# Attention scores of both heads issued together, one head in each half of TensorE's rows

## The reference

```
# stick-breaking, per head and block of 128 queries
z = q @ k.T * scale;  mask = key_pos < q_pos
log_beta = log_sigmoid(z);  log_1m = where(mask, log_sigmoid(-z), 0)
suffix = cumsum(log_1m, reverse=True) - log_1m
out = where(mask, exp(log_beta + suffix), 0) @ v
# global
out = softmax(q @ k.T * scale) @ v
# window: 128 keys to either side, bias by distance, one sink logit a head
s = q @ k.T * scale + bias;  m = max(max(s), sink);  p = exp(s - m)
out = (p / (sum(p) + exp(sink - m))) @ v
# neighbourhood: per grid row of 64 tokens, all 8 rows' keys in 16 columns
out = softmax(q @ k.T * scale + rpb[...]) @ v
```

## Time and profile before

| | us |
|---|---|
| median of 3 runs | 2117.64 (2117.27 to 2120.7) |
| profiled execution | 2116.69 |
| its span, first to last instruction | 2114.8 |
| PE busy | 2027.3 (96%), 8940 matmuls |
| VectorE busy | 1150.7 (54%) |
| ScalarE busy | 804.2 (38%) |
| GpSimd busy | 131.6 (6%) |
| mean granted TensorE clock | 0.980 |

### The profile page before, as it was taken

How to read it: one execution, slowest core, us unless ns; L and a number is a source line. 1 busy time by engine, 2 the same in 40 slices (tenths; PEclk the granted TensorE clock), 3 DMA queues, 4 the chain that set the end, 5 groups by cost and what they waited for, 6 DMA issues and landing times.

```text
span 2114.8 us, 26021 instructions
## 1 busy us (share of the span) xinstructions
PE 2027.3 (96%) x8940; PEld 1529.5 (72%) x8940; DVE 1150.7 (54%) x1991; ACT 804.2 (38%) x1402; POOL 131.6 (6%) x223
## 2 busy tenths in 40 slices
PE   6998999999999999999999997999898999999987
PEld 6875888888886665788888885565576866675766
DVE  6576534334456667444434465667754457677543
ACT  5456422222334445332212342544533333344331
POOL 1100000000000000000000000000003024342000
PEclk9998999999999999999999998999999999999998
DMA  6422232323321111223322320111222223222221
GB/s 215 148 80 70 90 100 92 117 80 98 100 87 54 58 52 50 82 90 99 109 81 98 102 88 31 40 55 50 65 68 84 79 68 79 69 75 65 79 73 69
DMA packets 48346, 173.78 MB, mean 82 GB/s; under 512 B 7344, under 2 KB 9408, under 8 KB 48016
## 3 DMA queue, kind: packets, MB, share of 16 engines
q1 hardware_dynamic: 41184, 160.45, 23.1%
q0 software_dynamic: 7088, 12.37, 2.4%
HBM read 168.58 MB, written 4.21 MB: 82 GB/s over the span
## 4 chain that ended last, share of the span: by engine, by line
PE 88%; DVE 7%; ACT 3%; issue 2%; DMA 1%; POOL 0%; DVEq 0%; ACTq 0%; SPq 0%; POOLq 0%
PE ps L366 25%; PE ps L368 23%; PE ps L367 23%; PE ps L458 7%; PE ps L488 3%; PE ps L466 3%; PE ps L549 1%; DVE Wl L1055 1%; PE ps L475 1%; ACT Wh L719 1%; DVE stat L1184 1%; DVE scr L1181 1%; DMA nmask<-in_nmask 1%; PE ps L435 0%; PE ps L401 0%
## 5 line engine op out<-in xcount | busy, mean ns | idle before, releaser
L366 PE MATMUL ps<-Hh,Wh 128*128 128x512 f32 x1568 | 641.4, 409 | 0.0
L368 PE MATMUL ps<-Hh,Wl 128*128 128x512 f32 x1568 | 613.3, 391 | 0.0
L367 PE MATMUL ps<-Hl,Wh 128*128 128x512 f32 x1568 | 612.9, 391 | 0.0
L719 ACT ACTIVATE Wh<-Wr 128x1024 fp32r<-128x1024 f32 (+2 forms) x276 | 308.9, 1119 | 709.1 <-PE ps L368 696.6
L1055 DVE TENSOR_TENSOR Wl<-Wr,Wh 128x1024 fp32r<-128x1024 f32 (+2 forms) x276 | 359.5, 1302 | 254.5 <-ACT Wh L719 254.4
L366 PEld LDWEIGHTS ps<-Hh,Wh 128*128 128x128 f32 x1568 | 294.7, 188 | 140.9 <-issue 84.2
L368 PEld LDWEIGHTS ps<-Hh,Wl 128*128 128x128 f32 x1568 | 294.8, 188 | 64.6
L367 PEld LDWEIGHTS ps<-Hl,Wh 128*128 128x128 f32 x1568 | 295.4, 188 | 55.4 <-issue 0.7
L366 PE MATMUL ps<-Yh,Wh 128*128 128x512 f32 (+1 forms) x800 | 305.0, 381 | 30.5 <-DVE Yl L1085 16.6
L367 PE MATMUL ps<-Yl,Wh 128*128 128x512 f32 (+1 forms) x800 | 301.0, 376 | 0.0
L368 PE MATMUL ps<-Yh,Wl 128*128 128x512 f32 (+1 forms) x800 | 300.5, 376 | 0.0
(11 more groups left out here) (175 smaller groups left out, 1596.2 us busy)
## 6 DMA issues: line engine op xcount, KB each, us to landing
Wr<-in_w SPq DMA_DIRECT2D x228, 512.0 KB, 3.4
Wr<-in_w SPq DMA_DIRECT2D x32, 768.0 KB, 4.2
Wr<-in_w SPq DMA_DIRECT2D x16, 640.0 KB, 3.9
scr<-in_rpb POOLq DMA_DIRECT2D x128, 24.0 KB, 2.0
X<-in_x SPq DMA_DIRECT2D x1, 2048.0 KB, 13.8
scr<-in_wri POOLq DMA_DIRECT2D x4, 512.0 KB, 3.8
out_t<-X SPq DMA_DIRECT2D x8, 256.0 KB, 2.1
scr<-d_rel POOLq DMA_DIRECT2D x8, 192.0 KB, 3.4
```

Source lines behind the costliest of these rows:

```text
L366: pe.matmul(bank[:, 0:n], hi, rh[:, k, :], start=(k == 0), stop=False)
L367: pe.matmul(bank[:, 0:n], hi, rl[:, k, :], start=False, stop=False)
L368: return pe.matmul(bank[:, 0:n], lo, rh[:, k, :], start=False, stop=(k == kc - 1))
L719: act.activation(Wh[:, slot, 0:kc * P], Wr[:, slot, 0:kc * P], ACT.Copy).then_inc(w_hi, 1)
```

## The change

Steps are reordered: `head_block` makes step `j` head `j % 2` and block `j // 2` (the memory attention keeps its order and gets a function of its own, `mem_scores`, with the wait of before). `scores` does nothing in an odd step; in an even one it issues the scores of both heads, head 0 in the array's rows 0 to 63 into `ps[2]`, head 1 in rows 64 to 127 into `ps[3]`, 512 keys as two cuts of 256. It waits for the exp of step g-1 (`t_e` at g), in the window stage for the bias add of step g-1. `Em` gets a second buffer by the parity of the pair, laid into `sq` and `ht`, so that GpSimd may write a pair's masks when the pair two before is done.

```
+def head_block(kind, j):
+    return (j // 4, j % 4) if kind == MEMA else (j % 2, j // 2)
...
-        Em = part(10240 + 2 * BW, 2, 8 * 112)
+        Em0 = part(10240 + 2 * BW, 2, 8 * 112)
+        Em = [[Em0[:, 0, :], Em0[:, 1, :]], [sq.rearrange("p a b -> p (a b)")[:, 0:8 * 112],
+                                             ht.rearrange("p a b -> p (a b)")[:, 0:8 * 112]]]
...
-            def mask_bias(i, hp):
+            def mask_bias(i, hp, par):
                 pool.wait_ge(en_in[hp], 128 * i + 128)
-                pool.wait_ge(sb_ok, 8 * i + (28 + 4 * hp))
+                pool.wait_ge(sb_ok, 8 * i + (23 + hp))
...
-            with pool.Fori(1, 8) as i:
-                for hp in range(2):
-                    pool.wait_ge(em_ok, 6 * i + (3 * hp - 3))
-                    load_bias(2 * i + hp, hp)
-                    mask_bias(i, hp)
+            pool.wait_ge(acc_ok, SQUARES["odd"] + KD)
+            with pool.Fori(0, 3) as it:
+                next_bias(2 * it + 1, 1)
+                next_bias(2 * it + 2, 0)
+            next_bias(7, 1)
...
             def scores(kind, g, par, j, grp=0):
-                h, b = j // 4, j % 4
-                lo, hi = 64 * h, 64 * h + 64
-                bank = ps[2 + j % 2]
+                if j % 2:
+                    return
+                b = j // 2
                 if kind == WIN and g >= STEP0["win"] + 2:
-                    pe.wait_ge(sb_ok, g - STEP0["win"] - 1)
+                    pe.wait_ge(sb_ok, g - STEP0["win"])
                 else:
-                    wait(pe, t_e, g - 1)
+                    wait(pe, t_e, g)
                 cs = key_chunks(kind, b)
                 k0, k1 = cs[0] * P, (cs[-1] + 1) * P
...
+                cuts = (k0, k0 + 256, k1) if k1 - k0 == S else (k0, k1)
+                for c0, c1 in zip(cuts, cuts[1:]):
+                    for h in range(2):
+                        lo, hi = 64 * h, 64 * h + 64
+                        keys = {GQA: KT[lo:hi, grp, c0:c1], WIN: KT2[lo:hi, grp, c0:c1]}.get(kind, KT[lo:hi, par, c0:c1])
+                        mm = pe.matmul(ps[2 + h][:, c0 - k0:c1 - k0], QT[lo:hi, par, b * P:(b + 1) * P], keys,
+                                       start=True, stop=True)
+                        if c1 == k1:
+                            mm.then_inc(t_s, 1)
...
-                            if jj % 4 == 0:
-                                wait(act, t_av, 2 * i + (g0 // 4 + jj // 4 - 1))
+                            if jj < 2:
+                                wait(act, t_av, 2 * i + (g0 // 4 + jj - 1))
                             copy_t(kind, g - 2, jj)
...
-                        if kind == NBR and j % 4 == 0:
-                            dve.wait_ge(em_ok, 6 * i + (3 + 3 * (j // 4)))
-                        before_exp(seg, kind, g, j)
+                        if kind == NBR and j < 2:
+                            dve.wait_ge(em_ok, 6 * i + (3 + 3 * j))
+                        before_exp(seg, kind, g, j, par=par)
```

More of the change, by code:

```diff
@@ L341, in mask_bias @@
                     n = w // 16
-                    pool.tensor_tensor(Em[:, hp, 8 * off:8 * (off + w)].rearrange("p (n k c) -> p n k c", n=n, k=8),
+                    pool.tensor_tensor(Em[par][hp][:, 8 * off:8 * (off + w)].rearrange("p (n k c) -> p n k c", n=n, k=8),
                                        e3[:, :, lo:hi].rearrange("p k (n c) -> p n k c", n=n),
@@ L345, in mask_bias, with next_bias @@
                                        .to_broadcast([P, n, 8, 16]), ALU.add).then_inc(em_ok, 1)
+            def next_bias(i, par):
+                for hp in range(2):
+                    pool.wait_ge(em_ok, 6 * i + (3 * hp - 3))
+                    load_bias(2 * i + hp, hp)
+                    mask_bias(i, hp, par)
             pool.wait_ge(sb_ok, 32)
@@ L439, in scores, with mem_scores @@
             def scores(kind, g, par, j, grp=0):
-                h, b = j // 4, j % 4
-                lo, hi = 64 * h, 64 * h + 64
-                bank = ps[2 + j % 2]
+                if j % 2:
+                    return
+                b = j // 2
                 if kind == WIN and g >= STEP0["win"] + 2:
-                    pe.wait_ge(sb_ok, g - STEP0["win"] - 1)
+                    pe.wait_ge(sb_ok, g - STEP0["win"])
                 else:
-                    wait(pe, t_e, g - 1)
+                    wait(pe, t_e, g)
                 cs = key_chunks(kind, b)
                 k0, k1 = cs[0] * P, (cs[-1] + 1) * P
[L449 to L458, removed]
+                cuts = (k0, k0 + 256, k1) if k1 - k0 == S else (k0, k1)
[7 more added lines that the diff above has]
+                            mm.then_inc(t_s, 1)
+            def mem_scores(g, par, j):
+                h, b = head_block(MEMA, j)
+                wait(pe, t_e, g - 1)
+                pe.matmul(ps[2 + j % 2][:, 0:MEM], (QT, KT2)[par][:, h, b * P:(b + 1) * P], memKa[:, 2 * par + h, :],
+                          start=True, stop=True).then_inc(t_s, 1)
             def turn(kind, g, j):
@@ L606, in mem_heads @@
                         g = g0 + 8 * i + j
-                        scores(MEMA, g, i, j)
+                        mem_scores(g, i, j)
                         q = first_q + 4 + 2 * i
@@ L783, in exps @@
             def exps(kind, g, j, i=0):
-                width = P * len(key_chunks(kind, j % 4))
+                h, b = head_block(kind, j)
+                width = P * len(key_chunks(kind, b))
                 bank, x = ps[2 + j % 2], j % 4
@@ L794, in exps @@
                 if kind == WIN:
-                    act.activation(stat[:, 4, j:j + 1], v_col("sink", 2 * i + j // 4), ACT.Exp, bias=stat[:, 1, j:j + 1])
+                    act.activation(stat[:, 4, j:j + 1], v_col("sink", 2 * i + h), ACT.Exp, bias=stat[:, 1, j:j + 1])
                 if kind in (WIN, NBR):
@@ L1148, in ffn, with before_exp @@
                 out_proj(f"down{layer}b", nrm)
[L1151 to L1153 removed]
+            def before_exp(seg, kind, g, j, i=0, par=0):
+                h, b = head_block(kind, j)
+                bank, x = ps[2 + j % 2], j % 4
                 w = P * len(key_chunks(kind, b))
@@ L1175, in before_exp @@
                         off = {0: P}.get(b, 0)
-                        bias = Ew[:, 2 * (i % 2) + j // 4, off:off + w]
+                        bias = Ew[:, 2 * (i % 2) + h, off:off + w]
                     else:
@@ L1179, in before_exp @@
                         off = (0, 32, 32, 80)[b]
-                        bias = Em[:, j // 4, 8 * off:8 * off + w]
+                        bias = Em[par][h][:, 8 * off:8 * off + w]
                     dve.scalar_tensor_tensor(Pb[:, x, 0:w], src, DH ** -0.5, bias, ALU.mult, ALU.add).then_inc(sb_ok, 1)
```

21 lines of the change are left out of this document (10 added, 11 removed).

## The result

The changed kernel takes 2126.76 us (median of 6 runs, 2121.22 to 2127.12), beside 2117.55 for the kernel before on the same chip (6 runs, 2116.94 to 2120.7). The ratio is 1.0035, 95% interval 1.0022 to 1.0048: slower by 0.35%, outside the 0.2% band. I had forecast 2110 and put 0.46 on faster. The time lies in the range of 2092 to 2138, 1.8 us from the centre of rival C, which had 24%.

What follows compares the result with a forecast made beforehand. PE, busy 96% of the span, was taken as the bound except in the window stage (VectorE). Stick -28, global +6, window -3 and neighbourhood +17 sum to -8: 2116.7 - 8 + 1 = 2110 us, range 2092 to 2138.

Steps and rivals of the forecast that it cites:

- rival C: Global and neighbourhood stages: TensorE's clock falls to 1.2 GHz after new waits; 2118 to 2132 us, likeliest 2125, slower; 24%.
- What the early issue costs, the neighbourhood stage: Neighbourhood stage: scores wait for a chain through the splits; 36.8 us for 34.46 a head pair, stage +17.
- rival B: Paired scores: the row halves don't overlap; 2162 us, or 2136 half-overlapped; 10%.
- The quarter of 0.21 us: Paired 512-wide scores: strict program-order starts would leave a quarter uncovered, 0.21 us; the prediction held row evidence against it.
- rival A: Whole kernel: PE is the bound throughout, as its 96% busy time suggests; 2037 us; 6%.
- Masks and second buffer, 0: Neighbourhood stage: GpSimd's masks move to the turn of pairs and cost 0, bounds -1 to +1 us a head pair.
- -28 + 6 - 3 + 17: Whole kernel: sum of the stick, global, window and neighbourhood terms, -8 us.
- The stick term, -28: Stick stage: PE stays the bound, 25.2 us for 28.94 a head pair, -28 us in all.
- the term of 0.41: Each score on PE: time around its columns, 0.2 + 0.11 + 0.1 = 0.41 us, saved four times a head pair.
- +2.3 and +2: Neighbourhood stage: +2.3 us for a full head pair, +2 for the last, with one product group a step as cover.
- The window, -3: Window stage: VectorE is the bound; scores ahead of the values product save half of 1.6 us idle each, -3 us.
- The global stage at full clock: Global stage: scores wait for the exp chain behind the splits; +6 us, where PE alone would give -20.

Runs made afterwards that it cites:

- a3_split_deferred: The changed kernel with VectorE's weight split moved from the even step to the following odd step in the global, window and neighbourhood stages: 2040.01 us, ratio 0.9638.
- a1_order_only: The changed kernel with its block order and second bias buffer, but each step issuing one head's scores with the old release: 2116.61 us, ratio 0.9997.
- a2_filled_waits: The changed kernel with one extra unused 0.85 us product ahead of even steps' score waits in global and neighbourhood stages: 2113.75 us, ratio 0.9981.

## Why the prediction was wrong

Right, and shown:
- **What the early issue costs, the neighbourhood stage.** 36.8 forecast, 36.71 measured wherever the clock stays up, with the chain as written (the timeline above).
- **Overlap of row halves (rival B).** Full; the pair costs what one score cost. The quarter of 0.21 us that the prediction read out of the program order does not appear either: the records start in program order, and yet 6 to 7 ns apart.
- **The naive reading (rival A).** 2037 was the price of a PE that never waits, and a3_split_deferred, which moves VectorE's split and nothing else, takes 2040. The order L738, L1076, L1203 was the whole obstacle in the neighbourhood stage. That the two totals meet is in part luck: by the stages' values products a3_split_deferred gains 25.0 us in the stick stage, 9.5 in the global one, 16.5 in the window one and 26.3 in the neighbourhood one with the stretch ahead of it, where A had 30, 20, 0 and 30.
- **Masks and second buffer, 0.** a1_order_only: 34.40 against 34.46.

Wrong:
- **The step that failed is the choice between the forecast and rival C.** I found waits of 0.7 to 2.9 us by my own sum, priced all of them at 1.00 of the clock, so that the clock stands in -28 + 6 - 3 + 17 at nothing, and gave their effect on it 24%. The evidence that I set against it was misread. The 3.1 us idle in 24.6 of the window stage at 1.00 are no small pieces: 2.25 of them are one wait at the end of that stretch, and the half clock behind it falls into the next stretch, the one with 0.88. PE, same place, and the granted clock of what follows, all of before:

```profile
1515.99 0.44 PE L466 MATMUL ps<-ident,scr 128*128 128x128 f32 x2 [2.25 <-DVE scr L1206]
1516.53 4.07 PE L488 MATMUL ps<-scr 128*64 128x256 f32 x16
```

```profile
1516.80:1520.21 3.41, 3.41 (x16) 1.45 (x12) 1.05 (x5) 0.90 (x3) 0.00 (x0) 0.50 0.09 31
```

A wait of the size that I forecast, then 3.4 us at 0.50, and a values product of 4.07 us for the 2.37 of the earlier trace rows: the row spoke for C. Measured in the neighbourhood stage: 1.55 us for each 3.4 us stretch, in three of the five full pairs between 1722.28 and 1910.51, and two more by 1945.84: about 8 of its 21.5 us. Four in the global stage are up to 6 more of its 11.3 (the first full pair there took 34.65 for the 33.1 I had, at 0.95 of the clock: one stretch). Rival C had 1.7 us a stretch, a price that it gave without a row, and up to five and eight of them, likeliest 15 us in all; nine came, at 1.55 some 14 us. Its 2125 was 1.8 us off. a2_filled_waits shows the cause and takes 11 us back.
- **The stick term, -28 for -25.4.** A pair saved 3.46, not 3.77: what surrounds a score is 0.33 to 0.34 us, not 0.41. The neighbourhood stage, once PE-bound, gives the same number (3.49 by a1_order_only and a3_split_deferred), so the term of 0.41 from the earlier trace rows was mis-sized. Which of its three parts (0.2, 0.11, 0.1) a pair still pays, no run separates.
- **The end of the neighbourhood stage.** I had +2.3 and +2 for its last two stretches. Measured from values product to values product, 30.29 became 35.33 and 15.16 became 15.71: +5.6 together, of which two clock stretches are 3.1. At full clock the +4.3 was too much.
- **The window, -3 for -5.1,** although it has stretches at half clock too (0.93 and 0.96 above). I had halved the wait of 1.6 us behind the values product without a row that says so; nothing was run on that alone.
- **The global stage at full clock.** +6 forecast; 11.3 less up to 6.2 for four stretches leaves 5.1 or a little more: right.

Put together: near full clock the change is worth about 4 us (a2_filled_waits: ratio 0.9981, with two dips, some 3 us, left in the global stage), where my sum had 8. So the sum without the clock was close, and the clock alone turned the sign. It was too small a margin to forecast "faster" with 8 to 22 us for the clock on the other side. Between the profiled run and the median stand another 5.5 us; their mean clock is 0.969 or 0.970 for 0.972. That these are more stretches at half clock fits, but it is not shown, since only the quickest run has a trace.

## What to carry to other kernels

Taking work off an engine that is busy 96% of the time pays only as far as its next instruction is ready: where it isn't, the us come back as a wait, and on TensorE such a wait can cost twice, once as idle time and once in slow products behind it: here five of 29 waits of the neighbourhood stage did, and of seven alike four did. Price the second part at its measured size times a share of the waits, not at nothing. Look at what stands in program order between two instructions that the critical engine now needs together; here one VectorE subtraction, whose own input came late, stood between two maxima, and moving it by one step was worth 87 us. When a sum is small beside a known one-sided risk, the risk decides the sign.

## What the runs showed of the hardware

- Two fp32 products with 64 rows each, in the upper and lower half of the array's rows, run fully beside each other: a pair of 512 columns takes 1.06 us to the next product, one took 1.05; cut or uncut makes 0.06 us. (The Trainium skill, TensorE: Matmul & The Clock Gate, Part 3 on packing small matmuls, says that products in different row groups run side by side; these traces agree, with starts 6 to 7 ns apart.)
- Waits of 1.68 or 1.69 us were followed by 3.4 us at 1.2 GHz in four of seven head pairs, at 0.43 us a product for 0.23, which costs 1.55 us. The same wait with 0.85 us of work put into it (idle 0.83) was followed by none in the six pairs that have it. (The Trainium skill, TensorE: Matmul & The Clock Gate, Part 1, has idle gaps as what throws the array back to 1.2 GHz; these two traces agree in kind, with gaps shorter than those that it warns of, and here the measurement decides.)
- A change over from products to a score and back costs 0.33 to 0.34 us beside the score's columns: (28.93 - 25.47 - 2.13) / 4 in the stick stage, (34.40 - 30.91 - 2.13) / 4 in the neighbourhood stage.
